# Mixed values kept transposed over the queries, taken from PSUM by ScalarE and VectorE in turn, scaled in place by GpSimd

## The reference, cut to what matters

```python
def _mixers(hn, w_in, g_out_a, g_out_b, sink_a, rpb_b, w_out):
    proj = einsum('bsd,de->bse', hn, w_in)
    qa, ka, va, qb, kb, vb = split(proj, SPLITS, axis=-1)
    ...                                   # partial rotary on qa and ka
    oa = _window_attention(qa, ka, va, sink_a)              # 8 heads, 2 kv heads, blocks of 128
    ob = _neighbourhood_attention(qb, kb, vb, rpb_b)        # 8 heads, 8 rows x 16 columns
    merged = concatenate([_rmsnorm(oa, g_out_a), _rmsnorm(ob, g_out_b)], axis=-1)
    return einsum('bse,ed->bsd', merged, w_out)

def _encoder_layer(x, ...):
    x = x + _mixers(_rmsnorm(x, g_attn), ...)
    h = _rmsnorm(x, g_ffn).reshape(B * S, D)
    return x + _expert_choice_ffn(h, w_router, w_gate, w_up, w_down).reshape(B, S, D)
```

## Time and profile before

| what | value |
|---|---|
| median of 3 runs | 2486.14 us (2483.61 to 2487.29) |
| profiled execution: its time / its span | 2484.71 us / 2482.9 us |
| busy share of the span: PE, PEld, DVE, ACT, POOL | 98%, 88%, 67%, 59%, 7% |
| granted TensorE clock, mean | 0.991 of full |

### The profile page before, as it was taken

One profiled execution on the slowest core, in us unless ns is written; L12 is line 12 of the kernel. 1 busy time (PEld: TensorE's weight loads), 2 busy tenths in 40 slices (PEclk: granted clock), 3 DMA queues, 4 the chain that ended last, 5 costly groups with the idle time before them and its releaser, 6 DMA issues.

```text
span 2482.9 us, 43086 instructions
## 1 busy us (share of the span) xinstructions
PE 2434.5 (98%) x16395; PEld 2178.7 (88%) x16395; DVE 1673.5 (67%) x2432; ACT 1456.5 (59%) x2050; POOL 163.7 (7%) x172
## 2 busy tenths in 40 slices
PE   9999999999889999999999999999999999999997
PEld 7888877777579989899998989999998989999896
DVE  6355278854776767676666767666676767666677
ACT  4332189977555656556565656555565655656574
POOL 0000000000010101101010100101010110101010
PEclk9999999999989999999999999999999999999998
DMA  7353255354376767767676767767676776767696
GB/s 250 123 177 113 62 163 202 122 186 154 111 286 224 260 224 258 240 241 247 234 248 233 250 234 248 256 230 251 223 259 226 256 244 238 251 230 253 228 325 222
DMA packets 104549, 545.29 MB, mean 220 GB/s; under 512 B 11344, under 2 KB 19920, under 8 KB 54800
## 3 DMA queue, kind: packets, MB, share of 16 engines
q1 hardware_dynamic: 97072, 518.19, 59.6%
q0 software_dynamic: 7392, 25.96, 4.5%
HBM read 503.21 MB, written 40.89 MB: 219 GB/s over the span
## 4 chain that ended last, share of the span: by engine, by line
PE 69%; DVE 1%; DMA 1%; ACT 1%; issue 0%; POOL 0%; SPq 0%; DVEq 0%; ACTq 0%
PE ex_gate_ps L2043 16%; PE ex_up_ps L2043 16%; PE ex_gate_ps L2045 7%; PE ex_up_ps L2045 7%; PE ex_down_ps L2058 2%; PE ex_down_ps L2062 2%; PE ex_down_ps L2059 2%; PE ex_down_ps L2060 2%; PE ex_down_ps L2063 2%; PE ex_up_ps L2058 2%; PE ex_up_ps L2062 2%; PE ex_up_ps L2063 2%; PE ex_up_ps L2060 2%; PE ex_up_ps L2059 2%; DMA fi_x<-acc_scratch 1%; PE ex_turn_ps L2011 0%
## 5 line engine op out<-in xcount | busy, mean ns | idle before, releaser
L1879 DVE TENSOR_TENSOR ex_w_lo<-ex_w,ex_w_hi 128x2048 fp32r<-128x2048 f32 x384 | 879.8, 2292 | 440.5 <-ACT ex_w_hi L1775 437.1
L1775 ACT ACTIVATE ex_w_hi<-ex_w 128x2048 fp32r<-128x2048 f32 x384 | 733.4, 1910 | 208.7 <-PE ex_down_ps L2063 106.8
L2043 PE MATMUL ex_gate_ps<-ex_xt,ex_w_hi 128*128 128x384 f32 x2048 | 591.8, 359 | 0.7 <-DVE ex_xt L1885 0.7
L2043 PE MATMUL ex_up_ps<-ex_xt,ex_w_hi 128*128 128x384 f32 x2048 | 592.1, 359 | 0.0
L2045 PE MATMUL ex_up_ps<-ex_xt,ex_w_lo 128*128 128x192 f32 x2048 | 512.7, 250 | 0.0
L2045 PE MATMUL ex_gate_ps<-ex_xt,ex_w_lo 128*128 128x192 f32 x2048 | 512.7, 250 | 0.0
L2045 PEld LDWEIGHTS ex_gate_ps<-ex_xt,ex_w_lo 128*128 128x128 f32 x2048 | 391.1, 191 | 0.6
L2045 PEld LDWEIGHTS ex_up_ps<-ex_xt,ex_w_lo 128*128 128x128 f32 x2048 | 391.2, 191 | 0.0
L2043 PEld LDWEIGHTS ex_gate_ps<-ex_xt,ex_w_hi 128*128 128x128 f32 x2048 | 384.5, 188 | 1.6 <-issue 1.0
L2043 PEld LDWEIGHTS ex_up_ps<-ex_xt,ex_w_hi 128*128 128x128 f32 x2048 | 384.5, 188 | 0.0
L1797 ACT ACTIVATE ex_up_low<-ex_up_ps 128x384 f32<-128x384 f32 x128 | 62.9, 492 | 207.8 <-PE ex_up_ps L2045 207.8
(11 more groups left out here) (310 smaller groups left out, 4012.3 us busy)
## 6 DMA issues: line engine op xcount, KB each, us to landing
ex_w<-in_w_experts SPq DMA_DIRECT2D x384, 1024.0 KB, 4.8
pj_w<-in_w_in SPq DMA_DIRECT2D x54, 512.0 KB, 3.7
pj_xr<-in_xt SPq DMA_DIRECT2D x12, 512.0 KB, 6.0
o_scratch<-ld_out SPq DMA_DIRECT2D x24, 256.0 KB, 4.6
at_bias<-in_near_bias SPq DMA_DIRECT2D x4, 1536.0 KB, 8.8
q_p<-in_x SPq DMA_DIRECT2D x12, 512.0 KB, 4.5
acc_scratch<-k_p SPq DMA_DIRECT2D x12, 512.0 KB, 5.4
h_scratch<-q_p SPq DMA_DIRECT2D x12, 512.0 KB, 3.0
```

Of the source, the lines that this page charges most:

```text
L1775: act.activation(w_hi[:, c % SLOTS, :], w[:, c % SLOTS, :], ACT.Copy).then_inc(hi_w, 1)
L1879: dve.tensor_tensor(w_lo[:, c % SLOTS, :], w[:, c % SLOTS, :], w_hi[:, c % SLOTS, :].bitcast(F32), ALU.subtract).then_inc(lo_w, 1)
L2043: nc.tensor.matmul(out[:, b, 0:2 * CAP], w_hi[:, slot, f], xt[:, k, :, :].rearrange("p h c -> p (h c)"), start=k == 0, stop=False)
```

## The change

The mixed values, which come out of the product as head elements by queries, are no longer turned back. They are written over the queries of the same unit, whose place is free by then, and `mix` takes its left operand from there.

- In `attend` the copies out of `at_mixed` go to `keep.q`: even units by ScalarE, odd units by VectorE, from two banks. The reciprocals are widened by GpSimd to 128 x 128 (`at_wide`), turned on TensorE behind the flips of the same unit, and copied with them (a block of 64 columns more in both copies). GpSimd then multiplies the queries' place by them. The store to and the loads from `o_scratch` are gone. The scores have 4 banks, two of which (`ld_open`) `mix` goes on with; the flips have 3 places, the biases 2.
- The row blocks of `w_out` are loaded during attention. One is split at unit 80, four in the steps behind the last unit, three in `mix`; the first half of tile 0's product runs in those steps too.
- In `mix` no tile is turned or scaled ahead of its product. Each tile's product has two parts (A: window rows, B: neighbourhood rows) in three pairs of banks, and each part is scaled by its root when it is added (four `scalar_tensor_tensor` a tile for two `tensor_tensor`). The squares come from ScalarE (three pieces a tile), GpSimd adds them in two steps, and TensorE sums them over partitions with a column of ones (`tally`, four products for two tiles).

```diff
@@ attend: ScalarE
+                if 0 <= u - OUT < N and (u - OUT) % 2 == 0:
+                    v = u - OUT
                     act.wait_ge(weighed, v + 1)
-                    if v >= 2:
-                        act.wait_ge(o_turned, v - 1)
-                    act.activation(o_turn[:, v % 2, :], mixed_ps[:, 0:P], ACT.Copy).then_inc(o_copied, 1)
+                    act.activation(queries(v, slice(0, P)), mixed_ps[0][:, 0:P], ACT.Copy).then_inc(taken[0], 1)
...
@@ attend: GpSimd
+            def share(v):
+                pool.wait_ge(taken[v % 2], v // 2 + 1)
+                o = queries(v, slice(0, P))
+                pool.tensor_tensor(o, o, flipped[:, v % FLIPS, 2 * units[v][0].tiles, :], ALU.mult).then_inc(kept, 1)
+            for v in range(N):
+                pool.wait_ge(inverted, v + 1)
+                if v >= WIDES:
+                    pool.wait_ge(flipped_ps, 2 * (v - WIDES + 1))
+                pool.tensor_copy(wide[:, v % WIDES, :].rearrange("p (h e) -> p h e", h=2),
+                                 rden[:, v % STATS, :].unsqueeze(2).broadcast_to([P, 2, HD])).then_inc(widened, 1)
+                if v >= OUT - INVERT:
+                    share(v - OUT + INVERT)
...
@@ attend: VectorE
                 if 0 <= u - FLIP < N:
+                    v = u - FLIP
+                    dve.wait_ge(flipped_ps, 2 * v + 2)
+                    if v >= FLIPS:
+                        dve.wait_ge(kept, v - FLIPS + 1)
+                    dve.tensor_copy(flip_to(v, 1), flip_from(v, 1)).then_inc(copied[1], 1)
+                if 0 <= u - INVERT < N:
+                    v, r = u - INVERT, (u - INVERT) % STATS
                     dve.wait_ge(exped, 2 * v + 2)
                     dve.reciprocal(rden[:, r, :], sums[:, r, :]).then_inc(inverted, 1)
...
-                    dve.tensor_tensor(dst, own,
-                                      rden[:, r, :].unsqueeze(2).broadcast_to([P, 2, HD]),
-                                      ALU.mult).then_inc(scaled, 1)
+                if 0 <= u - OUT < N and (u - OUT) % 2 == 1:
+                    v = u - OUT
+                    dve.wait_ge(weighed, v + 1)
+                    dve.tensor_copy(queries(v, slice(0, P)), mixed_ps[1][:, 0:P]).then_inc(taken[1], 1)
...
+                if u == EARLY_SPLIT or N <= u < N + LEAD_SPLITS - 1:
+                    j = max(u - N + 1, 0)
+                    dve.wait_ge(lead.hi_w, j + 1)
+                    dve.scalar_tensor_tensor(out=lead.w_lo[j], in0=lead.w[j], scalar=shared.gain_out[:, j:j + 1],
+                                             in1=lead.w_hi[j].bitcast(F32), op0=ALU.mult,
+                                             op1=ALU.subtract).then_inc(lead.lo_w, 1)
@@ attend: TensorE
+                    pe.wait_ge(widened, v + 1)
+                    c = slice(2 * tiles * HD, (2 * tiles + 1) * HD)
+                    turned = [nc.tensor.transpose(flip_ps[i][:, c], wide[ROWS[i], v % WIDES, :], ident[ROWS[i], ROWS[i]])
+                              for i in range(2)]
                     for last in turned:
                         last.then_inc(flipped_ps, 1)
-                if u >= OUT:
-                    v = u - OUT
-                    pe.wait_ge(o_copied, v + 1)
-                    if v >= 1:
-                        pe.wait_ge(scaled, v)
-                    turned = [nc.tensor.transpose(out_ps[:, h, 0:HD], o_turn[ROWS[h], v % 2, :],
-                                                  ident[ROWS[h], ROWS[h]]) for h in range(2)]
-                    turned[1].then_inc(o_turned, 1)
...
@@ mix: ScalarE
+            for j in range(LEAD_SPLITS, DT):
                 split(j)
+                if j < DT - 1:
+                    square_mixed(j - LEAD_SPLITS)
             raise_m(1)
+            take_root1(0)
...
@@ mix: VectorE
                     if n < TILES:
                         lower(n)
+                add(s, A)
                 dve.wait_ge(routed, t + 1)
                 dve.tensor_reduce(neg_raw[:], bank[6][:, LOGITS], AX.X, ALU.max,
```

661 lines of the change are left out of this document (303 added, 358 removed).

## The result

| what | before | after |
|---|---|---|
| median of the runs of this comparison | 2484.92 us (6 runs, 2483.61 to 2487.29) | 2495.03 us (6 runs, 2492.55 to 2495.93) |
| profiled execution: its time / its span | 2484.71 / 2482.9 us | 2495.37 / 2493.6 us |
| ratio, 95% interval | | 1.0042 (1.0031 to 1.0053) |

The change makes the kernel 10.1 us slower. The forecast was 2487.6 in a range of 2480 to 2497: the range held, the likeliest case did not come. Rival 1 named nearly this time (2494.8), but for a cause that is not there.

What follows compares the result with a forecast made beforehand. TensorE, busy 98% of the span, was taken to bound the kernel. The terms +3.0 + 1.0 - 0.9 - 1.6 = +1.5 on 2484.71 gave 2486.2, and 1.43 for the median 2487.6 us; range 2480 to 2497.

Steps and rivals of the forecast that it cites:

- the likeliest case: Whole kernel: a median of 2487.6 us; this forecast case, about 2483 to 2491, was given 0.47.
- Rival 1: Attention: GpSimd's copy or handoffs slower than reckoned, each 0.1 us costing 3.6; with 0.2 more 2494.8 us; chance 0.25.
- TensorE's two new turns, and 384 keys unchanged: Attention: two transposes go and two come at 0.21, nothing won or lost; units of 384 keys stay at 2.07 us.
- The ring: Attention, 256 keys: widened reciprocals through GpSimd close a 3.31 us loop over two units, 1.65 against 1.53 each; 3.0 lost.
- The early split: Attention, unit 80: ScalarE and VectorE each get one whole row block; VectorE's idle time absorbs part of 1.281; 1.0 lost.
- The passage: From attention's last score to the mixer's second turned tile: 0.9 us won, bounded by 2.5 won and 0.7 lost.
- Middle tiles: Mixer: without turning a scaled tile the affinities start 0.37 us earlier, 8 times; 3.0 us won.
- The search tile: Mixer tile with a search in all three places: two more VectorE additions make it grow by about 1.4 us.
- Behind the eleventh turned tile: Last tile of the mixer: the search stands ahead of the addition before and after, so nothing.
- The 1.43 for the median: Whole kernel: the median of the runs lies 1.43 us above the profiled execution, taking 2486.2 to 2487.6.
- Rival 2: Attention's start: GpSimd's first product comes late behind a configuration; with 6 us in all, 4 lost, 2491.6; chance 0.08.
- Rival 3: Faster: new turns at 0.04 for 0.21, ring hidden, no split blocked, search tile has room; 2479.6 us; chance 0.2.

Runs made afterwards that it cites:

- the doubled copy: The changed kernel with GpSimd copying each unit's reciprocals twice, first to a place nobody reads: 2503.64 us, ratio 1.0083.
- the two kernels without a split: Changed kernel with no split among attention's units, plus other mends: 2485.29 us; the same with part of the first two tiles' sum of squares left out: 2484.42 us.
- the kernel that lets it be measured: Against the kernel with no split among attention's units (2485.29 us), GpSimd adds no squares for the first two tiles, result wrong: 2484.42 us, ratio 1.0004.

## Why the prediction was right in its range and wrong in its steps

- **TensorE's two new turns, and 384 keys unchanged:** right, 2.08 before and after, though by only 0.08 of slack.
- **The ring, +3.0:** mechanism right, shown by the doubled copy; mis-sized. GpSimd's copy is 0.29 for 0.30, and it follows the reciprocals by 0.06, not 0.18; the whole ring of 3.31 came out all the same (424.55 to 427.86). The units of 256 keys lost 0.06 each, not 0.12, since they had taken 1.58 and not the 1.53 of one pair: between units 48 and 60 attention loses 0.5. As much or more, 0.84 in the kernel after, is lost in the first six units, while the pipeline fills; in six of the other kernels it is 0.4 with the same code there. Together 1.75 to 2.07 by the two kernels without a split.
- **The early split, +1.0:** failed. By the whole of attention it costs 4.26 (184.70 less 180.44), by the gaps behind it 4.1. I weighed VectorE's 1.281 against its idle time, as if its half lay anywhere. I did not ask what it waits for: ScalarE's half in the same step, which takes 1.14 and comes behind that step's exponentials. Of the 4.1 the order makes 3.0 and the work 1.1 (0.9 among units of 384 keys): the 1.0 was right for the work, and the step that failed is the overlap. Nor did I see that this split has two inputs from SBUF: the sentence that VectorE has one at most in attention leaves it out.
- **The passage, -0.9 (at worst +0.7):** wrong in sign and outside its bounds, +2.72. Its parts that go away did go (from the second tile's first product to its turned `x2` 22.57 before, 514.68 to 537.25, and 19.68 after). But the tail grew by 5.61: the wait ahead of the last flips with the half clock behind it (2.1 by mending it), the boundary of the stages in the middle of the splits (1.8 by mending it alone), and the clash with GpSimd. I had priced only the last (up to 1.9; 1.0 reached TensorE in the kernel that lets it be measured). The row that I read as a sign of the clash, a `TENSOR_SCALAR` of 2.10, has one input from SBUF and not two, so it did not bear out the rule as I told it; the splits and low halves do (1.28 to 2.14, 1.36 to 2.98).
- **Middle tiles, -3.0:** wrong, they gave nothing (+0.4). The idea holds, they wait for the affinities; but these began 5.59 us behind the turn of `x2` in place of 5.81, since the low half began 2.99 behind it in place of 2.36 and the addition held them. That is 0.14 a tile for my 0.37, and `tally` takes 0.35 back in every second tile, for which I had put in nothing.
- **The search tile, +1.4:** 14.19 for 13.69, +0.5.
- **Behind the eleventh turned tile:** put in at nothing, +0.85. Of this 0.15 is the last tile; the rest I can't pin down: the stretch behind it took 33.75 to 34.74 in kernels whose code there is the same (33.81 before).
- **The range:** it held by luck. Its upper edge stood there for rival 1, and the likeliest case was 9.2 us short on the profiled execution: 2.3 in attention, 3.6 in the passage, 3.4 in the middle tiles and 0.85 behind them, less 0.9 at the search tile. The 1.43 for the median came from three runs; over six it is 0.21.
- **Rival 1 (GpSimd's chain slower):** refuted, copy and handoffs are 0.06 + 0.29 + 0.06 for 0.53 (at 471.65); its time came by chance. **Rival 2 (a late start of GpSimd):** refuted, the first product follows the copy of 323.75 at 324.10. The Trainium skill's first-call cost of some 6 us (GPSIMD Engine Reference, Instruction dispatch) is not seen here. **Rival 3:** its free turns did not come.

Open: why a middle tile that waits for nothing takes 13.28 where 13.68 less the turned tile's 0.59 would be 13.09; what makes one early gap of attention 2.10 in one kernel and up to 2.64 in another with the same code; and whether GpSimd's product, which frees the places of the flips, has a share in what the ring costs.

## What to carry to other kernels

Work tucked into a pipelined loop is priced by what it waits for in its own step and by what queues behind it, not by its length against an engine's idle share: where a piece has two halves on two engines, try the second a step later (4.1 us of loss became 1.1 here). A boundary that all engines leave together, set in the middle of a chain of work, idles the engines of that chain. Where a hole on TensorE stands near it, mend both before you judge either: with only the boundary mended, the low clock grew from 6.8 to 10.2 us. Before work goes to an idle GpSimd, look for the VectorE instructions with two SBUF inputs that will run at the same time. And compare stretches of several profiles: a gap that differs with no edit looks like a gain.
